# Two weight sums of the first seven-product pair by accumulating DMAs, in a two-block transformer kernel on one core

## The reference, cut to what matters

```
hf = rms_norm(x, norm_ffn)
gate, up = split(hf @ w_ffn_in)          # 1024 -> 2 * 2816
x = x + (silu(gate) * up) @ w_ffn_out    # 2816 -> 1024
return rms_norm(x, norm_final)
```

## Time and profile before

| | |
|---|---|
| median of 3 runs | 1569.22 us (1568.54 to 1569.37) |
| the profiled execution | 1569.12 us, of which the span of the records is 1567.3 us |
| PE / DVE / ACT / POOL busy in the span | 99% / 64% / 44% / 4% |
| mean granted TensorE clock | 0.998 |
| DMA | 161 MB, 103 GB/s on average |

### The profile page before, as it was taken

How to read it: one execution, slowest core, us unless ns; L and a number is a source line. 1 busy time by engine, 2 the same in 40 slices (tenths; PEclk the granted TensorE clock), 3 DMA queues, 4 the chain that set the end, 5 groups by cost and what they waited for, 6 DMA issues and landing times.

```text
span 1567.3 us, 20924 instructions
## 1 busy us (share of the span) xinstructions
PE 1551.4 (99%) x7916; PEld 1315.4 (84%) x7916; DVE 1004.7 (64%) x1605; ACT 693.0 (44%) x1161; POOL 68.2 (4%) x58
## 2 busy tenths in 40 slices
PE   9999999999999999999999999999999989999998
PEld 7877777888888888888888888888888889989987
DVE  6776878666644545357786545465655889848735
ACT  5455776643322222264444334344444445524414
POOL 0000000020000000040000010010002000000002
PEclk9999999999999999999999999999999999999999
DMA  5333232342222322223442232334123223332322
GB/s 193 125 102 99 84 93 76 101 136 100 95 98 91 107 95 94 95 94 114 132 130 65 75 134 88 115 122 148 54 83 106 94 95 109 108 108 82 113 83 74
DMA packets 54035, 160.99 MB, mean 103 GB/s; under 512 B 6960, under 2 KB 8368, under 8 KB 53808
## 3 DMA queue, kind: packets, MB, share of 16 engines
q1 hardware_dynamic: 53632, 159.14, 31.0%
q10 hardware_dynamic: 304, 0.52, 0.1%
HBM read 148.11 MB, written 2.10 MB: 96 GB/s over the span
## 4 chain that ended last, share of the span: by engine, by line
PE 95%; DVE 2%; DMA 1%; ACT 1%; issue 1%; DVEq 0%; SPq 0%; ACTq 0%
PE G L1230 73%; PE SC L1230 7%; PE TP L1230 6%; PE O L1230 4%; PE M L1230 3%; PE TP L1653 1%; PE TP L1599 1%; DMA RAW<-in_f 1%; DVE WL L2274 0%; DMA GN<-in_gains 0%; PE TP L1702 0%; ACT WH L1740 0%; ACT MGh L1740 0%; DMA RAW<-in_fg 0%; DVE WTl L2274 0%
## 5 line engine op out<-in xcount | busy, mean ns | idle before, releaser
L1230 PE MATMUL G<-XGh,WH 128*128 128x512 f32 x984 | 388.6, 395 | 0.0
L2274 DVE TENSOR_TENSOR WL<-RAW,WH 128x1024 fp32r<-128x1024 f32 (+2 forms) x277 | 302.8, 1097 | 131.5 <-ACT WH L1740 131.1
L1230 PE MATMUL G<-XGh,WL 128*128 128x512 f32 x984 | 383.6, 390 | 0.0
L1230 PE MATMUL G<-XGl,WH 128*128 128x512 f32 x984 | 383.2, 389 | 0.0
L1740 ACT ACTIVATE WH<-RAW 128x1024 fp32r<-128x1024 f32 (+2 forms) x283 | 256.9, 913 | 152.9 <-PE G L1230 108.7
L1230 PEld LDWEIGHTS G<-XGh,WH 128*128 128x128 f32 x984 | 184.8, 188 | 41.3 <-issue 3.8
L1230 PEld LDWEIGHTS G<-XGh,WL 128*128 128x128 f32 x984 | 184.7, 188 | 39.3
L1230 PEld LDWEIGHTS G<-XGl,WH 128*128 128x128 f32 x984 | 184.9, 188 | 36.3
L1230 PE MATMUL G<-MGh,WH 128*128 128x512 f32 x372 | 145.0, 390 | 0.0
L1230 PE MATMUL G<-MGl,WH 128*128 128x512 f32 x372 | 144.7, 389 | 0.0
L1230 PE MATMUL G<-MGh,WL 128*128 128x512 f32 x372 | 144.7, 389 | 0.0
(11 more groups left out here) (420 smaller groups left out, 2759.8 us busy)
## 6 DMA issues: line engine op xcount, KB each, us to landing
RAW<-in_up SPq DMA_DIRECT2D x32, 512.0 KB, 3.2
RAW<-in_dn SPq DMA_DIRECT2D x32, 512.0 KB, 3.2
RAW<-in_fg SPq DMA_DIRECT2D x22, 512.0 KB, 4.6
RAW<-in_g SPq DMA_DIRECT2D x16, 512.0 KB, 3.2
RAW<-in_f SPq DMA_DIRECT2D x16, 512.0 KB, 3.6
X<-in_x SPq DMA_DIRECT2D x16, 256.0 KB, 4.4
RAW<-in_q SPq DMA_DIRECT2D x8, 512.0 KB, 3.3
RAW<-in_k SPq DMA_DIRECT2D x8, 512.0 KB, 3.4
```

Source lines behind the costliest of these rows:

```text
L1230: return e.matmul(dst, st, mv, start=start, stop=stop, skip_group_check=True)
L2274: return e.tensor_tensor(dst, src, hi.bitcast(F32), ALU.subtract)
```

## The change

Three things are changed. First, for the first pair (f = 6) t1 and t3 are no longer summed by DVE. SP loads b11 into T[4] and b12 into T[5], and when these have landed GpSimd issues four accumulating DMAs (the step fetch_add) which add b12 to T[4] and b22 to T[5] from HBM, each in two halves of 64 partitions. Those loads stand early in the list, at index 7, behind the load of fg 3. The tile sums 0 and 2 of this pair are gone, and with them the forced settling ahead of them. Second, the load of b22 is an entry of its own (b22), so that the load into t3 (sums) has a wait of its own, without that of place 2. Third, the residual tiles f0 and f1 take places in the order PLACES = 0, 3, 1, 2, 0, 2, 0, 1, where place 3 is T[4:6], the sum buffers of the even pairs; the tiles f2 go to (n + 2) mod 3.

In the list of loads this gives, with the number of rounded items that each waits for (before / after): sums 6: 22 at index 12 / 8 at index 7; b22 of 6: 22 / 22; pair 6: 24 / 24; sums 7: 22, then s_lo / s_lo alone; f0 tile 0: 87 / 87; tile 1: 94 / 87; tile 2: 94 / 94; tile 3: 96 / 94; tile 4: 98 / 96; tile 5: 100 / 102; tile 6: 102 / 104; tile 7: 104 / 104 (behind tile 6). For f1 the same holds with 58 more.

```diff
-SUM_AT = (0, 1, 2, 5)
+SUM_AT, ADDED, EARLY = (0, 1, 2, 5), 1, 7
+PLACES = (0, 3, 1, 2, 0, 2, 0, 1)
...
-                out.append(("sums", n, 2, max(behind, held.get(2, 0)) if new else behind))
+                behind_2 = max(behind, held.get(2, 0)) if new else behind
+                if new and n % 2 == 0:
+                    behind = max(behind, held.get(3, 0))
+                if n == DIRECT:
+                    out.insert(EARLY, ("sums", n, 2, out[EARLY - 1][3]))
+                else:
+                    out.append(("sums", n, 2, behind))
+                out.append(("b22", n, 2, behind_2))
                 out.append(("pair", n, side, max(behind, held.get(side, 0))))
                 held[side] = q + 7
+                if side == 0:
+                    held[3] = q + 7
...
-                third = (len(self.units) + n_plain) % NRAW if name in ("fg", "fu") else n % NRAW
+                if name in ("fg", "fu"):
+                    third = (len(self.units) + n_plain) % NRAW
+                else:
+                    third = PLACES[n] if name != "f2" else (n + 2) % NRAW
...
             self.put("fetch", self.fetched)
+            name, f = self.fetches[self.fetched][:2]
+            if name == "sums" and f < DIRECT + ADDED:
+                self.put("fetch_add", f)
...
             if name == "st" and j in SUM_AT:
-                if (f, j) == (DIRECT, 0):
-                    self.settle(self.rounded)
-                self.put("tile_sum", f, SUM_AT.index(j))
+                i = SUM_AT.index(j)
+                if f >= DIRECT + ADDED or i in (1, 3):
+                    self.put("tile_sum", f, i)
...
+        def raw_tile(third):
+
+            return RAW[:, third, :] if third < NRAW else T[:, 4:6, :].rearrange("p a s -> p (a s)")
...
+                        if TURN7[n] < ADDED:
+                            e.dma_start(b["t1"], a["fg"][n][:, 0:S]).then_inc(d_b11[n % 2], 16)
                         e.dma_start(b["t3"], a["fu"][n][:, 0:S]).then_inc(d_b12[n % 2], 16)
-                        e.dma_start(b["b22"], a["fu"][n][:, S:2 * S]).then_inc(d_b22[n % 2], 16)
+                    elif name == "b22":
+                        e.dma_start(b_tiles(n)["b22"], a["fu"][n][:, S:2 * S]).then_inc(d_b22[n % 2], 16)
...
                         if part == 0:
-                            e.wait_ge(t_sum, 4 * TURN7[n] + 1)
+                            if TURN7[n] < ADDED:
+                                e.wait_ge(t1_added[TURN7[n]], 32)
+                            else:
+                                e.wait_ge(t_sum, SUMMED["tile_sum", n, 0])
...
+                elif kind == "fetch_add":
+                    f = arg[0]
+                    b, n = b_tiles(f), TURN7[f]
+                    for tile, loaded, added, more in (("t1", d_b11[f % 2], t1_added[n], slice(0, S)),
+                                                      ("t3", d_b12[f % 2], t3_added[n], slice(S, 2 * S))):
+                        e.wait_ge(loaded, X_LOAD + 16)
+                        for r in (slice(0, P // 2), slice(P // 2, P)):
+                            e.dma_start(b[tile][r, :], a["fu"][f][r, more], accum_op=ALU.add).then_inc(added, 16)
...
                     elif i == 1:
-                        e.wait_ge(t_sum, 4 * n + 1)
+                        if n < ADDED:
+                            e.wait_ge(t1_added[n], 32)
+                        else:
+                            e.wait_ge(t_sum, SUMMED["tile_sum", f, 0])
                         e.wait_ge(d_b22[f % 2], X_LOAD + 16 * (n // 2 + 1))
                         e.tensor_tensor(b["t2"], b["t1"], b["b22"], ALU.add).then_inc(t_sum, 1)
```

More of the change, by code:

```diff
@@ L1074, in program @@
         i_hi, i_lo, i_done = sem("i_hi"), sem("i_lo"), sem("i_done")
-        d_b12, d_b22 = d_x[0:2], d_x[2:4]
+        d_b12, d_b22, d_b11 = d_x[0:2], d_x[2:4], d_x[4:6]
+        LOADED = (*d_raw, d_x[6])
+        t1_added, t3_added = ([sem(f"{n}{i}") for i in range(ADDED)] for n in ("t1_added", "t3_added"))
+        SUMMED = tally("tile_sum")
         X_LOAD = 32
@@ L1081, in program @@
         TURN7 = {f: k for k, f in enumerate(pairs)}
-        RAW_LOADS, n = {}, [sum(1 for v in range(len(units)) if v % NRAW == third) for third in range(NRAW)]
+        RAW_LOADS, n = {}, [sum(1 for v in range(len(units)) if v % NRAW == third) for third in range(NRAW)] + [X_LOAD // 16]
         for i, (name, _, third, _) in enumerate(fetches):
-            if name != "sums":
+            if name not in ("sums", "b22"):
                 n[third] += 1
@@ L1149, in _ @@
                             e.wait_ge(prep_dve, PREP_DVE["s_lo", 3])
+                        if TURN7[n] < ADDED:
+                            e.dma_start(b["t1"], a["fg"][n][:, 0:S]).then_inc(d_b11[n % 2], 16)
                         e.dma_start(b["t3"], a["fu"][n][:, 0:S]).then_inc(d_b12[n % 2], 16)
-                        e.dma_start(b["b22"], a["fu"][n][:, S:2 * S]).then_inc(d_b22[n % 2], 16)
+                    elif name == "b22":
+                        e.dma_start(b_tiles(n)["b22"], a["fu"][n][:, S:2 * S]).then_inc(d_b22[n % 2], 16)
                     else:
                         c = 768 if name == "f2" else 1024
-                        e.dma_start(RAW[:, third, 0:c], a["fg" if name == "pair" else name][n]).then_inc(d_raw[third], 16)
+                        e.dma_start(raw_tile(third)[:, 0:c], a["fg" if name == "pair" else name][n]).then_inc(LOADED[third], 16)
                 elif kind == "stack":
@@ L2153, in _ @@
                         elif part == 3:
-                            e.wait_ge(t_sum, 4 * TURN7[n] + 3)
+                            if TURN7[n] < ADDED:
+                                e.wait_ge(t3_added[TURN7[n]], 32)
+                            else:
+                                e.wait_ge(t_sum, SUMMED["tile_sum", n, 2])
                         elif part == 5:
@@ L2157, in _ @@
                         elif part == 6:
-                            e.wait_ge(t_sum, 4 * TURN7[n] + 4)
+                            e.wait_ge(t_sum, SUMMED["tile_sum", n, 3])
                     else:
                         third = next(x[2] for x in fetches if x[:2] == (name, n))
-                        src = RAW[:, third, part * S:part * S + c]
-                        e.wait_ge(d_raw[third], 16 * RAW_LOADS[name, n])
+                        src = raw_tile(third)[:, part * S:part * S + c]
+                        e.wait_ge(LOADED[third], 16 * RAW_LOADS[name, n])
                     hi(item_tile(q)[0], src).then_inc(i_hi, 1)
@@ L2841, in _ @@
                             e.wait_ge(i_lo, taken("st", f - 2, 0))
-                            e.wait_ge(t_sum, 4 * n - 6)
-                        elif n == 1:
-                            e.wait_ge(prep_dve, PREP_DVE["s_lo", 3])
+                            e.wait_ge(t_sum, SUMMED["tile_sum", f - 2, 1])
                         e.wait_ge(d_b12[f % 2], X_LOAD + 16 * (n // 2 + 1))
@@ L2852, in _ @@
                     elif i == 2:
-                        e.wait_ge(t_sum, 4 * n + 2)
+                        e.wait_ge(t_sum, SUMMED["tile_sum", f, 1])
                         e.tensor_tensor(b["t3"], b["t3"], b["b22"], ALU.add).then_inc(t_sum, 1)
                     else:
-                        e.wait_ge(t_sum, 4 * n + 3)
+                        if n < ADDED:
+                            e.wait_ge(d_raw[f % 2], 16 * RAW_LOADS["pair", f])
+                        e.wait_ge(t_sum, SUMMED["tile_sum", f, 3] - 1)
                         e.tensor_tensor(b["t4"], b["t2"], b["b21"], ALU.add).then_inc(t_sum, 1)
```

2 lines of the change are left out of this document (1 added, 1 removed).

## The result

| | before | after |
|---|---|---|
| median | 1569.3 us (8 runs, 1568.54 to 1569.65) | 1564.78 us (8 runs, 1563.37 to 1565.66) |
| ratio | | 0.997, 95% interval 0.996 to 0.9981 |
| profiled execution, span | 1569.12, 1567.3 us | 1565.65, 1563.9 us |

The change gains 4.5 us, 0.3%. The eight runs of the changed kernel fall into two groups by their mean granted clock: 1563.37, 1563.64, 1563.99 and 1564.21 at 0.999, and 1565.36, 1565.36, 1565.65 and 1565.66 at 0.998. The profiled one is of the second group. It is the times that tell the groups apart; the mean clock is only a hint, because it also holds the end of the program, where PE has no work left and the granted clock goes to 0.50 (in this profile for the last 2.9 us), and that stretch is longer in some executions than in others.

A forecast was written before the change was run, and what follows sets the result against it. PE was taken as the bound, busy 99%, with three holes holding 8.3 us. Gains of 1.6 + 1.5 + 1.4 + 1.1 = 5.6 us off the profiled 1569.12, with medians 0.1 higher, gave 1563.6 us, range 1562.4 to 1566.2.

The forecast's parts named there:

- The replay of DVE's list: DVE's steps from block 4's epilogue to pair 7's first sum: block 5's first multiplication 1.6 us earlier, at 1267.4.
- the last hole: PE's wait for one_out before pair 6's fifth product: shrinks from 4.24 to 2.6 us but does not close.
- The clock term: Pair 6's fifth and sixth products: PE's clock no longer falls after the shorter idle time, 1.5 us gained.
- the sign of being wrong that I had named: A PE clock of 0.50 after the wait at pair 6, named among the signs against the forecast.
- the likeliest case: Whole kernel: all gains come, clock at pair 6 staying up; 1562.9 to 1564.4 us, 58%.
- the first rival: Behind pair 6's hole the clock falls all the same: gain 4.1 us, 1565.1 us, 18%.
- Holes two and three: PE's waits for one_out at pairs 15 and 21: both close as f0's tile 1 loads earlier, 1.4 and 1.1 us.
- Loads, adds and Pool's issuing at nothing: Moved loads, accumulating DMAs for pair 6 and Pool's four issues from 1220 on: taken to cost 0 us.
- the upper end of 2.1 us: Pool's four issues blocking DVE near 1220 as long as adds: PE loses up to 2.1 us; rival given 6%.
- Slower: From 1220 on Pool holds DVE much longer; at 4 us per issue 1576.3 us, 3%.
- hole one: PE idle before pair 6's fifth product, 4.24 us: shortened by 1.6 us as DVE runs earlier.

The follow-up runs named there:

- the repeat: The changed kernel measured again with no edit, beside its own runs of the kernel before: 1565.34 us, ratio 0.997.
- before again: The kernel before with no edit, profiled a second time: 1569.91 us.
- before, third: The kernel before with no edit, profiled a third time: 1569.31 us.
- places put back: The changed kernel with residual tiles f0, f1 and f2 back in their old places, none in T[4:6]: 1565.86 us, ratio 0.998.
- the idle sums: The changed kernel with two unused sums and the settling given back to DVE, without the wait for the gate tile: 1564.9 us, ratio 0.9974.
- the later adds: The changed kernel with pair 6's early loads at index 12 of the list instead of 7: 1565.5 us, ratio 0.9974.

## Why the prediction was right, and where it was not

Predicted were 1563.6 us with a range of 1562.4 to 1566.2; measured 1564.8.

*The replay of DVE's list* was right to 0.1 us: block 5's first multiplication at 1267.4 (1267.35 on the old scale), the first sum of pair 7 at 1272.0 (1271.95), a hole of 2.6 (2.58). The limit seen there, that the chain over DVE and ACT to one_out is longer than PE's four half products, is what the last hole is made of: with ACT's order changed it goes.

*The clock term*, 1.5 us gained, is the step that failed in more than half of the runs. I put 2.4 us of idle time to the 1.13 that left the clock alone, as the nearer row. By the two groups the clock fell in 4 of the first 8 runs and in 6 of the repeat's 7, the profiled ones among them, and filling the hole prices it at 1.75 us. In the profile the sign of being wrong that I had named, a low clock behind the hole, is there. So the likeliest case and the first rival (1565.1, given 18%) are both seen, the rival more often; the first median lies between them. A row that lies between two bounds was no ground for 58 against 18.

*Holes two and three*, 1.4 and 1.1 us: the mechanism was right, the size was one profile's. The other profiles of the same pattern show waits of 1.1 (before again), 2.0 (before, third) and 0.6 us (places put back), and the times give 0.8 to 0.9 for closing them. The term of 2.5 was over double of what it is worth.

*Loads, adds and Pool's issuing at nothing*: right. That the adds run one after another, which the prediction had as its upper bound, is what they do. The first reader of t1 is not DVE at 1260, as I had it, but ACT, at 1255.92 in the profile; and from the bound of 1241.7 to 1260 it is 18 us, not 19. Neither changes the term. No new hole shows in PE between 1220 and 1240, and a remainder of DVE took the same 1.22 us right beside an issue, as in the timeline of DVE of the changed kernel,

```profile
1229.42 1.22 DVE L2315 TENSOR_TENSOR WTl<-RAW,WTh 128x1024 fp32r<-128x1024 f32 x1
```

so the upper end of 2.1 us did not come: this remainder ran at the same time as the issue of 1229.38 to 1230.20 and was not held.

The prediction also priced the issues by a rule of the Trainium skill (SBUF — State Buffer, section SBUF: two separate sides), and left out a condition of it: for a VectorE operation with two SBUF inputs the rule holds only against a GpSimd operation that reads SBUF. The Trainium skill, Perfetto Trace Analysis, section DMA Instruction — SWDGE (GPSIMD), says that such a DMA instruction reads no tensor, so by the two pages together the rule would not reach these issues. The trace agrees in so far as the remainder was not held; no run here shows that this is the reason.

*Slower*: Pool holding DVE has no trace here. Where adds do lose (the second pair), it is by coming late, against which the prediction saw ample time for the first pair.

*The total* owes something to luck. What the experiments show is 1.66 us for hole one and 0.8 to 0.9 for the late holes, which makes 2.5, and 1.6 to 1.75 more where the clock stays up, some 4.2. The medians gain 4.5, in the repeat too, where all runs but one are of the group of higher times. So a late-hole term that was too large, and a clock term that mostly did not come, were made up for by something that no term of the prediction holds.

What stays open is that something, up to 2 us in the repeat. One place of it can be seen. PE's wait that ends at 296.27 in the first profile of the kernel before ends at 296.40 and 297.74 in its other two, and at 296.13 to 296.89 in the profiles of the changed kernel and its variants. The second profile of the kernel before (1569.91 us, close to the medians of its chip) and that of the repeat (1565.10) are 4.81 us apart, and 1.43 of these lie ahead of that wait, where the change has touched nothing. Whether the kernel before has such late starts more often, or whether this is the chance of three profiles, is not shown. The mean clock of 0.996 in many of its runs is no proof of more low clock while PE works, as the end of the program counts in it. Open are also the last 0.9 us of waits at pairs 7 and 8, and whether one add over all 128 partitions, in place of two halves that follow one another, would make adds quick enough for a second pair.

## What to carry to other kernels

Where a wait goes from an in-order queue, replay the queue up to the next place where it waits for the engine that bounds: what is earlier there is the gain, and a wait and the work behind it don't add (0.7 and 0 alone, 1.66 together). Size a hole that hangs on the landing of one load from several executions, not from one. Compare runs that fall into groups group with group; a median only says which group was the more common. A hole as long as one after which the clock sometimes falls costs more than its length: close it, or, as here, fill it with work that nobody reads. Use accumulating DMAs for tiles that have time to spare: several of them cost one landing after another.

## What the hardware showed that was not expected

TensorE's clock fell to the 1.2 GHz level behind an idle time of 2.42 us in four profiles (the changed kernel, its repeat, the idle sums, the later adds) and stayed at 2.4 GHz behind an idle time of 2.42 us at the same place in a fifth (the old places). In the run with two pairs by adds it fell behind each of the idle times of 2.74 and 2.24 us; behind those of 1.13, 1.20 and 1.43 it never did. In the profile of the changed kernel it fell only after PE had restarted: 1.00 in the idle stretch, 0.62 and 0.53 in the two behind.

An accumulating DMA of 64 partitions from HBM is busy on Pool for 0.81 to 0.98 us, lands 2.8 to 6.0 us after its issue, and the next one starts 3.2 to 6.3 us after it. The last two go together: in all ten profiles with such DMAs, 33 times, the next one starts 0.2 to 0.4 us after the one before has landed, though the kernel puts no wait between the two halves of a tile. So they run one at a time; whether the chip or the compiled program makes them do so is not shown. The Trainium skill, Perfetto Trace Analysis, section DMA Instruction — SWDGE (GPSIMD), says that the profiled time of such an instruction is the making of its descriptors and not the movement of the data. The trace agrees, as the landing comes after the instruction's end, and the idle time of Pool between two of them, put down to "issue" in the rows above, is the rest of that landing.
